# DeepNorm hybrid layer on one Trainium2 core: the first gate by seven half-size products inside the attention stage, the output gate's tiles in halves in the recurrence

## What is computed

```python
proj = x @ w_in
cq, ckv, kr, f_pre, q_pre, i_pre, g_pre, ga, gb = split(proj)      # ga, gb: 1024 columns each, g_pre: 512
a = attention(...)           # latent attention, softmax over earlier chunks (prompt) or a cache (sample)
o, S = hgrn2(...)            # gated linear recurrence over f, q, i
o = rms(o) * hg_norm * silu(g_pre)
merged = sigmoid(ga) * (a @ w_br_a) + sigmoid(gb) * (o @ w_br_b)
x = layernorm(ALPHA * x + merged @ w_out)
x = layernorm(ALPHA * x + mixture_of_experts(x) + sigmoid(x @ w_ple_gate) * (p @ w_ple))
```

## Time and profile before

| | us |
|---|---|
| median of 3 runs | 1517.29 (1516.72 to 1517.4) |
| profiled execution, device time | 1517.23 |
| its span, first to last instruction | 1515.5 |
| PE busy / DVE / ACT / POOL | 1273.6 / 453.6 / 287.0 / 62.8 |
| mean granted clock of TensorE | 0.918 |

### The profile page before, as it was taken

One profiled execution on the slowest core, in us unless ns is written; L12 is line 12 of the kernel. 1 busy time (PEld: TensorE's weight loads), 2 busy tenths in 40 slices (PEclk: granted clock), 3 DMA queues, 4 the chain that ended last, 5 costly groups with the idle time before them and its releaser, 6 DMA issues.

```text
span 1515.5 us, 21258 instructions
## 1 busy us (share of the span) xinstructions
PE 1273.6 (84%) x8912; PEld 738.4 (49%) x8913; DVE 453.6 (30%) x1109; ACT 287.0 (19%) x710; POOL 62.8 (4%) x102
## 2 busy tenths in 40 slices
PE   7999999999787767767799999999987876677664
PEld 4866897544332323322277679866442332333221
DVE  4552654532111101011166446445211111011003
ACT  3443422021001101001044434212111011000001
POOL 1300010000000000000040010000000000000000
PEclk9999999999899878788899999999998898778787
DMA  9503675999999999999972147679999999999994
GB/s 335 166 0 112 219 184 196 420 363 429 428 430 430 429 431 430 429 431 427 388 254 84 36 146 215 185 271 374 420 430 430 428 431 432 430 427 430 431 425 170
DMA packets 82643, 497.22 MB, mean 328 GB/s; under 512 B 7472, under 2 KB 13552, under 8 KB 51952
## 3 DMA queue, kind: packets, MB, share of 16 engines
q1 hardware_dynamic: 75392, 476.47, 76.7%
q0 software_dynamic: 7152, 19.32, 5.4%
HBM read 488.67 MB, written 2.89 MB: 324 GB/s over the span
## 4 chain that ended last, share of the span: by engine, by line
PE 57%; DMA 35%; DVE 3%; SPq 3%; issue 1%; ACT 1%; POOL 0%; DVEq 0%
PE bank L1105 55%; DMA ring<-in_w_e_up 7%; DMA ring<-in_w_e_down 5%; DMA ring<-in_w_e_gate 5%; DMA arena<-in_w_e_up 4%; DMA cst<-in_w_e_down 4%; DMA arena<-in_w_e_gate 4%; DMA cst<-in_w_e_gate 3%; DMA arena<-in_w_e_down 2%; SPq L924 2%; PE bank L1155 2%; DMA ring<-in_w_in 1%; SPq L985 0%; DVE arena L2304 0%; DVE arena L2144 0%
## 5 line engine op out<-in xcount | busy, mean ns | idle before, releaser
L1105 PE MATMUL bank<-arena 128*32 128x512 f32 (+11 forms) x2808 | 572.4, 540 | 169.6 <-DMA ring<-in_w_e_up 51.6
L1105 PE MATMUL bank<-ring,arena 128*32 128x512 f32 (+4 forms) x1360 | 422.2, 649 | 36.1 <-DMA arena<-in_w_e_gate 16.9
L1105 PEld LDWEIGHTS bank<-arena 128*32 128x32 f32 (+6 forms) x2808 | 210.5, 137 | 436.6 <-issue 422.9
L1105 PE MATMUL bank<-ring,xT 128*32 128x128 f32 (+5 forms) x1536 | 237.2, 363 | 1.3 <-ACT xT L1732 1.1
L1105 PEld LDWEIGHTS bank<-ring,xT 128*32 128x32 f32 (+1 forms) x1536 | 121.4, 137 | 100.6 <-issue 90.1
L1105 PEld LDWEIGHTS bank<-ring,arena 128*32 128x32 f32 (+1 forms) x1360 | 107.8, 130 | 123.1 <-issue 115.6
L1105 PE MATMUL bank<-xT,ring 128*128 128x144 f32 (+1 forms) x640 | 113.4, 335 | 0.0
L1105 PEld LDWEIGHTS bank<-xT,ring 128*128 128x128 f32 x640 | 95.1, 190 | 12.3
L1105 PE MATMUL bank<-arena,x_sb 128*128 128x128 f32 (+1 forms) x768 | 99.7, 282 | 1.4 <-DVE arena L2526 0.8
L1105 PEld LDWEIGHTS bank<-arena,x_sb 128*128 128x128 f32 (+1 forms) x768 | 90.5, 190 | 19.4 <-issue 12.7
L1105 PE MATMUL bank<-cst,arena 128*32 128x512 f32 x144 | 90.7, 789 | 0.0
(11 more groups left out here) (253 smaller groups left out, 1018.2 us busy)
## 6 DMA issues: line engine op xcount, KB each, us to landing
arena<-in_w_e_up SPq DMA_DIRECT2D x30, 2048.0 KB, 27.8
arena<-in_w_e_gate SPq DMA_DIRECT2D x28, 2048.0 KB, 27.1
ring<-in_w_e_gate SPq DMA_DIRECT2D x24, 2048.0 KB, 25.4
arena<-in_w_e_down SPq DMA_DIRECT2D x20, 2048.0 KB, 23.9
ring<-in_w_e_down SPq DMA_DIRECT2D x18, 2048.0 KB, 24.9
ring<-in_w_in SPq DMA_DIRECT2D x32, 1024.0 KB, 9.2
ring<-in_w_e_up SPq DMA_DIRECT2D x16, 2048.0 KB, 24.6
arena<-in_w_e_gate SPq DMA_DIRECT2D x16, 1024.0 KB, 14.4
```

The source lines that it names most:

```text
L1105: return pe.matmul(out, lhsT, rhs, start=first, stop=last, skip_group_check=True)
```

## The change

The first gate `ga` is made by the seven products too, in the attention stage: products 4 and 5 at the place of the output gate's first tile, 3 and 2 at that of the second, 7 and 1 behind the sample scores, 6 ahead of "lat". Their order is 4, 5, 3, 2, 7, 1, 6. POOL sums its weights by four accumulating DMAs behind the cache loads. Since its results need the room, the turned cache `cT` moves to the buffer of the forget gate and is loaded last, after the forget gate has been used. The output gate's tiles 0 and 1 go to four places of the recurrence's first tile, in halves of four matmuls (`HALF_AT` for first halves); its tile 2 stays. Product places of gb move up by one: each of the seven now has a place of its own. The ring's order of pieces changes: uq ahead of i, ga ahead of g.

```diff
-GATE_AT = {("ss",): [("ga", 0), ("ga", 1)], ("lat",): [("ga", 2)],
-           ("A", 0, 1): [("ga", 3)], ("A", 0, 3): [("ga", 4)], ("ks", 0): [("ga", 5)], ("o", 0): [("ga", 6)],
-           ("A", 1, 1): [("ga", 7)], ("A", 1, 3): seven_of("gb", 4), ("ks", 1): seven_of("gb", 5), ("o", 1): seven_of("gb", 3),
-           ("A", 2, 0): seven_of("gb", 2, 1), ("ks", 2): seven_of("gb", 7), ("o", 2): seven_of("gb", 6)}
+GATE_AT = {("at", 0): seven_of("ga", 4, 5), ("at", 1): seven_of("ga", 3, 2), ("ss",): seven_of("ga", 7, 1), ("lat",): seven_of("ga", 6),
+           ("A", 0, 3): [("g", 0)], ("o", 0): [("g", 1)],
+           ("A", 1, 1): seven_of("gb", 4), ("A", 1, 3): seven_of("gb", 5), ("ks", 1): seven_of("gb", 3), ("o", 1): seven_of("gb", 2),
+           ("A", 2, 0): seven_of("gb", 1), ("ks", 2): seven_of("gb", 7), ("o", 2): seven_of("gb", 6)}
+HALF_AT = {("A", 0, 1): 0, ("ks", 0): 1}
+SEVEN_ORDER = {"fq": SEVEN, "gb": SEVEN, "ga": (4, 5, 3, 2, 7, 1, 6)}
...
-    out += [(name, h) for name in ("cq", "kv", "f", "q", "i") for h in range(2)]
-    out += [("uq", 0), ("uq", 1), ("uk", 0), ("uv", 0)]
+    out += [(name, h) for name in ("cq", "kv", "f", "q") for h in range(2)]
+    out += [("uq", 0), ("uq", 1), ("i", 0), ("i", 1), ("uk", 0), ("uv", 0)]
+    out += [("ga", j, h) for j in range(2) for h in range(2)]
     out += [("g", 0), ("g", 1)]
-    out += [(name, j, h) for name in ("ga", "gb") for j in range(2) for h in range(2)]
+    out += [("gb", j, h) for j in range(2) for h in range(2)]
...
-    j += [("S", 1, n) for n in range(4)] + [("aT", 0), ("g", 0)] + [("PT", 1, kt, h) for kt in range(2) for h in range(2)]
-    j += [("ql",), ("aT", 1), ("i", 2), ("qlT",), ("g", 1)]
+    j += [("S", 1, n) for n in range(4)] + [("aT", 0)] + GATE_AT["at", 0] + [("PT", 1, kt, h) for kt in range(2) for h in range(2)]
+    j += [("ql",), ("aT", 1), ("i", 2), ("qlT",)] + GATE_AT["at", 1]
...
-        cT = carve(later_gates, 2, PAST)
-        wukT = carve(later_gates + 2 * PAST, HEADS, 2, 128)
+        cT = carve(H + 6144, 2, PAST)
+        wukT = carve(later_gates + T * FEATURES // 2, HEADS, 2, 128)
...
-                pool.dma_start(cT[:, :, :], cache_turned[layer]).then_inc(cache_in, 16)
...
+                pool.wait_ge(lf_out, 2 * (layer + 1))
+                pool.dma_start(cT[:, :, :], cache_turned[layer]).then_inc(cache_in, 16)
...
+                ns, w = quarters("ga")
+                pool.wait_ge(ring_full[SIGNAL_OF[ns[0, 1]]], 16 * FILLS[ns[0, 1]])
+                pool.dma_start(w[0, 1], from_input("ga", 1, 1), accum_op=ALU.add).then_inc(ga_sum[7], 16)
+                job_done(pool, (layer, "ga", 4, 1))
+                pool.dma_start(w[0, 0], from_input("ga", 0, 1), accum_op=ALU.add).then_inc(ga_sum[2], 16)
+                job_done(pool, (layer, "ga", 5, 1))
+                pool.wait_ge(ga_sum[2], 16 * (layer + 1))
+                pool.dma_start(w[1, 1], w[0, 0], accum_op=ALU.add).then_inc(ga_sum[1], 16)
+                job_done(pool, (layer, "ga", 3, 1))
+                pool.wait_ge(ga_sum[1], 16 * (layer + 1))
+                pool.dma_start(w[1, 0], w[1, 1], accum_op=ALU.add).then_inc(ga_sum[6], 16)
...
+                    if place in HALF_AT:
+                        project_half(layer, ("g",), HALF_AT[place], xT, [("g", 0), ("g", 1)], 0)
                     for name, *f in GATE_AT.get(place, []):
-                        if name == "gb" and len(f) == 2:
+                        if name == "g":
+                            project_half(layer, ("g",), f[0], xT, [("g", 0), ("g", 1)], 1)
+                        else:
                             seven((layer, name, *f), piece_number(layer, (name,) + SEVEN_WEIGHTS[f[0]]))
-                        else:
-                            by_features(layer, (name, f[0]), f[0] % 4, [(name, f[0] // 4, 0), (name, f[0] // 4, 1)], xT)
...
-                combined("g", (0,))
+                gates_at("at", 0)
...
-                combined("g", (1,))
+                gates_at("at", 1)
...
@@ ScalarE @@
-                        if name == "gb":
-                            if f[0] in (4, 5, 3):
-                                seven_copies(key, gb_copied)
-                            continue
-                        job_done(act, key)
-                        emptied(act.copy(dict(ga=gate_a, gb=gate_b)[name][f[0]], bank(key)[:, 0:T]), key)
+                        if name == "g":
+                            projected("g", hg, f[0], ACT.Copy)
+                        elif f[0] in (4, 5, 3):
+                            seven_copies((layer, name, *f), ga_copied if name == "ga" else gb_copied)
...
@@ VectorE @@
+                    if i == 1:
+                        gates_at("at", 0)
                     for kt in range(i + 1):
                         key = (layer, "PT", i, kt, 1)
                         job_done(dve, key)
                         emptied(dve.tensor_copy(probT[:, kt, 4:8, :], bank(key)[:, :].rearrange("p (h t) -> p h t", h=4)), key)
+                gates_at("at", 1)
...
+                gates_at("ss")
...
-                levels(0)
+                longer_sums(0, 0)
+                products(0, 0)
+                gates_at("lat")
+                levels(0, 1)
```

More of the change, by code:

```diff
@@ L709, in build @@
         hq_out = sem("hq_out")
+        ga_sum = {m: sem(f"ga_sum_{m}") for m in SUMS}
+        ga_copied = sem("ga_copied")
         gb_sum = {m: sem(f"gb_sum_{m}") for m in SUMS}
@@ L1045, in _, with quarters, from_input @@
                     pool.dma_start(kT[QK:QK + 2, h, :], masks[1]).then_inc(mask_in, 16)
+                pool.wait_ge(lf_out, 2 * (layer + 1))
+                pool.dma_start(cT[:, :, :], cache_turned[layer]).then_inc(cache_in, 16)
+                def quarters(name):
+                    ns = {(j, h): piece_number(layer, (name, j, h)) for j in range(2) for h in range(2)}
+                    return ns, {at: slot(n).rearrange("p (c n) -> p c n", c=4) for at, n in ns.items()}
+                def from_input(name, j, h):
+                    a = OFF[name][0] + 512 * j
+                    return w_in[layer].rearrange("(p c) n -> p c n", c=8)[:, 4 * h:4 * h + 4, a:a + 512]
+                ns, w = quarters("ga")
[9 more added lines that the diff above has]
+                pool.dma_start(w[1, 0], w[1, 1], accum_op=ALU.add).then_inc(ga_sum[6], 16)
                 job_done(pool, (layer, "ss", 2))
@@ L1050, in _ @@
                 pool.memset(att[:, :, :], 0.0).then_inc(zeroed, 1)
-                ns = {(j, h): piece_number(layer, ("gb", j, h)) for j in range(2) for h in range(2)}
-                w = {at: slot(n).rearrange("p (c n) -> p c n", c=4) for at, n in ns.items()}
-                def from_input(j, h):
-                    a = OFF["gb"][0] + 512 * j
-                    return w_in[layer].rearrange("(p c) n -> p c n", c=8)[:, 4 * h:4 * h + 4, a:a + 512]
+                ns, w = quarters("gb")
                 job_read(pool, (layer, "aTs"))
@@ L1181, in seven @@
                     pe.wait_ge(forms_out, layer + 1)
+                    if key[1] == "ga" and m in SUMS:
+                        pe.wait_ge(ga_sum[m], 16 * (layer + 1))
                     if key[1] == "gb" and m in SUMS:
@@ L1882, in _ @@
                 read_attended(0)
-                projected("g", hg, 0, ACT.Copy)
+                gates_at("at", 0)
                 read_probs(1)
@@ L1952, in gate_values @@
                     for k in pairs:
-                        if k < FEATURES // 2:
-                            for i in (2 * k, 2 * k + 1):
-                                job_read(act, (layer, "ga", i))
-                        else:
-                            job_read(act, (layer, "gb", 6 if k // 2 % 2 else 7, k % 2))
+                        name = "ga" if k < FEATURES // 2 else "gb"
+                        job_read(act, (layer, name, 6 if k // 2 % 2 else 1 if name == "ga" else 7, k % 2))
                         act.activation(gate_pair(k), gate_pair(k), ACT.Sigmoid).then_inc(early_gates, 1)
@@ L2209, in gather @@
                         dve.wait_ge(signal, copied(layer, m, p))
-                    job_read(dve, (layer, name, SEVEN[SEVEN.index(m) - 1], p))
+                    order = SEVEN_ORDER[name]
+                    job_read(dve, (layer, name, order[order.index(m) - 1], p))
                     for i, j, op in SEVEN_TO[m]:
@@ L2218, in gates_at @@
                     for name, *f in GATE_AT.get(place, []):
-                        if name == "gb" and f[0] != 4:
-                            gather((layer, name, *f), gb_copied)
+                        if name != "g" and f[0] != 4:
+                            gather((layer, name, *f), ga_copied if name == "ga" else gb_copied)
                 for t in range(3):
@@ L2402, in place_part, with levels @@
                         dve.sem_inc(att_out, 1)
-                def levels(t):
-                    for k in range(LEVELS[t]):
+                def levels(t, first=0):
+                    for k in range(first, LEVELS[t]):
```

21 lines of the change are left out of this document (13 added, 8 removed).

## The result

| | before | changed |
|---|---|---|
| median, 6 executions each | 1517.09 us (1516.37 to 1518.12) | 1507.06 us (1506.17 to 1507.89) |
| ratio | | 0.9932, 95% interval 0.9922 to 0.9942 |
| profiled execution, device time | 1517.23 | 1507.20 |
| span | 1515.5 | 1505.4 |

The change brings 10.0 us; 8.4 had been forecast (1508.8). In two later sessions the same kernel gave 1505.44 and 1508.01 us beside 1517.3 and 1517.8, gains of 11.9 and 9.8.

A forecast was written before the change was run, and what follows sets the result against it. Each layer was taken as a PE-bound part followed by a full expert-weight stream, with the change wholly in the first. Terms summed to -4.18 us a layer, -8.4 for two, so 1517.2 became 1508.8 us; range 1505.0 to 1513.0.

The forecast's parts named there:

- a microsecond behind 365 us is worth nothing: Expert stage: weights stream at full rate, so PE time saved there gains nothing; ahead of it, savings count one for one.
- attention, first and second place: Attention stage: two products, together 7.84 us, replace each output gate tile of 6.97 and 6.87 us; +0.87 and +0.97 us.
- wait for bank 0: Recurrence: PE's wait at the first level products for ACT to empty bank 0 goes; -0.25 us a layer.
- four half tiles: Recurrence: four output gate half tiles at 3.54 us replace four whole features, 14.16 for 15.67 us; -1.51 us a layer.
- wait before product 3: Recurrence: PE waits 1.14 us for DVE's gather of product 5, plus 0.16 restart; +1.30 us a layer, bounds 0 and 2.5.
- third tile's first place: Recurrence: product 1 alone at 3.92 us replaces products 2 and 1 with their 1.45 us wait, 9.54 us; -5.62 us a layer.
- Tile 0: Recurrence: slack of tile 0's attention weights before PE's outputs shrinks to 0.3 us; cost 0, up to 1 in the range.
- The sums: Attention stage: POOL's accumulating DMAs land in time, sum 2 with 5.7 us of slack before product 2; cost nothing.
- (1): Recurrence: DVE reaches the gather in time, no new wait; -5.5 us a layer, 1506.3 us, chance 0.17.
- (2): Recurrence: DVE becomes the bound and PE's shorter pieces turn into waits; -2.4 us a layer, 1512.4 us, chance 0.13.
- (3): Expert weights: their stream starts on something unmoved and absorbs the gain; 1515 to 1517 us, chance 0.07.
- (4): Attention stage: sum 2 is late and PE stands before product 2; at 22 us +2.8 a layer, 1522.8 us, chance 0.05.

The follow-up runs named there:

- e7: Changed kernel with the second branch's first feature made three times, +3.9 us of PE a layer just ahead of the expert weights; 1514.91 us, ratio 0.9984.
- e9: Kernel before with three branch features made from one of their four chunks each, 4.4 us of PE less a layer; 1508.52 us, ratio 0.9939.
- e10: Changed kernel with the second branch's first feature made twice, +1.96 us of PE a layer; 1510.99 us, ratio 0.9955.
- e8: Changed kernel with expert group 4's token gathering done twice, +6.4 us of PE a layer within the expert stream; 1508.46 us, ratio 0.994.
- e1_after: Changed kernel run again without any edit, as a yardstick; 1505.44 us, ratio 0.9922.
- e3: Changed kernel with all new places kept, but the first gate made by eight plain features without weight sums; 1517.07 us, ratio 0.9994.
- e6: Changed kernel without the first gate's four accumulating DMAs and PE's waits for them; 1505.56 us, ratio 0.9924.
- e2: Changed kernel with DVE's gather of second-gate product 5 moved ahead of tile 2's level 3, ACT's copies likewise earlier; 1503.26 us, ratio 0.9908.
- e4: Kernel before with first-gate feature 7 moved to "lat" and the second gate's product places moved up by one; 1515.44 us, ratio 0.9988.
- e11: Changed kernel run once more without any edit, on one chip with two other probes; 1508.01 us, ratio 0.9935.
- e5: Changed kernel with the accumulating DMA of the first gate's sum 2 issued twice, product 2 waiting for both; 1524.99 us, ratio 1.0053.

## Why the prediction was right

- **What bounds the kernel.** Confirmed by e7, e9 and e10, which moved the end by 9.5 for 7.8, 9.3 for 8.8 and 3.0 for 3.9 us of PE work in places with nothing of the gates. The sentence that a microsecond behind 365 us is worth nothing was only half right: in layer 0 of e8 the added work held nothing up, but the sentence left out PE's clock: the same block takes 7.11 or 8.80 us there, and the end moves with it. The waits on the chain are also not all "11 us and more": that of before has 11.32, 10.81 and 9.60 us one behind the other.
- **Terms of the sum, layer 0.** Measured as differences of starts on PE's timelines:

| term | forecast | measured |
|---|---|---|
| attention, first and second place | +0.87, +0.97 | +0.97, +0.97 |
| products 7 and 1, 6 | +0.02 | +0.12 |
| wait for bank 0 | -0.25 | -0.31 |
| four half tiles | -1.51 | -1.72 |
| first outputs | 0 | +0.10 |
| seventh place | +0.04 | +0.04 |
| wait before product 3 | +1.30 | +0.97 |
| third tile's first place | -5.62 | -5.61 |
| sum | -4.18 | -4.47 |

- Two terms were mis-sized by more than 0.1 us. The half tile is 3.49 us (13.95 for four), the value that half of the old tile had given; I had taken 3.54 between that and the output projection's. The wait was 0.93 instead of 1.14: DVE released the bank at G+18.0 as worked out (197.84 against G = 179.83, the start of the first outputs), but PE came at G+17.08 instead of 16.91, and the lost overlap was 0.07 instead of 0.16. Together they raise the gain by 0.54 us a layer. The first attention place, products 7, 1 and 6 and the first outputs take 0.1 us each of it back, and bank 0 gives 0.06. That leaves 4.47 a layer, 9.0 in all. The forecast's 8.4 against 10.0 is thus right in mechanism and a little small in size.
- **Layer 0 of this profile.** The terms add up to 4.47, yet the dense part is only 3.6 us shorter, because this execution took 0.85 us more from its first transpose to the first touched place (97.95 us against 97.10). The same kernel in e1_after took 97.19 there and is 4.4 shorter, so this is scatter ahead of the change.
- **Tile 0.** DVE's last copy of tile 0's weights ends at 179.72 and PE's outputs start at 179.83: of 0.3 us of slack 0.1 is left, and no wait, as had been taken. The outputs took 0.10 us more; e3 has this too, and its cause was not followed. **The sums.** Slack of sum 2 5.2 us against 5.7, cost nothing (e6). **The wait's place and cause.** As said; e2 took it away and got 2.2 us back.
- **What the forecast missed.** The gain of 9.8 to 11.9 in the medians is 1 to 3 us above these 9.0. The extra stands in the expert parts: their two stretches together are 1001.4 to 1002.0 us in the profiled executions of before, e3, e4 and e9, and 998.2 to 1000.4 in those of the changed kernel's kind (e8 apart). It isn't the earlier start, for e9 starts as early and has 1002.0. It is the clock of the two blocks told above. The forecast had taken this stage as the same in both kernels, which it is in bytes and work. Whether the change itself moves these blocks to the better is open. For it: the first block of layer 0 is slow in three of four profiles with eight gate features and in none of nine with seven products. Against it: one profile each, the last block of layer 1 is slow in the changed kernel's first profile too, and executions of one kernel scatter by 4 us (e11) to 5 us (e3, e7). The part of the gain beyond 9.0 us was not foreseen, and may be luck.
- **Rivals.** (1), no new wait, is what e2 built: its dense parts are 5.3 and 5.5 us shorter than before, close to the 5.5 worked out, and it ended at 1503.3, below the 1506.3, by its expert parts. The change itself has the wait, so this rival falls. (2), DVE as the bound: no, 0.1 us of slack held. (3), absorbed: no. (4), sum 2 late: did not occur, but its price was mis-sized. By my arithmetic an accumulate time of 20.8 us (9.15 and 11.67) would have left +1.6 us a layer against before; e5's dense parts show +4.7 and +6.1, and its median 7.4 in all against the 1517.6 beside it, because I had priced only the wait and not the lower clock behind it (2.9 and 2.5 us, and 1.7 more in layer 1).

## What to carry to other kernels

Find the point up to which PE paces the kernel and make the sum only ahead of it, piece by piece from start to start; here the terms added up to within 0.3 us a layer. Behind that point look at the blocks of PE work that stand between two waits for weights: their clock still moves the end, here by 1.3 to 2.2 us a block. When products move up by one place, follow each PSUM bank through the engine that empties it: here the wait did not vanish but went to another product, and moving one gather on DVE ahead of a level paid as much per layer as was waited. Price a wait on PE at its length plus what the following matmuls lose in clock; waits of 5.8 and 6.2 us cost another 2.9 and 2.5 here. Before a difference of 1 to 3 us in 1500 is given a cause, compare the pieces of several profiles.

## What the runs showed of the hardware

- After 5.78 us without work PE ran the next product in 7.00 us instead of 4.09, at a granted clock of 0.58; after 6.22 us in 6.58. After the waits of 0.93 us the product took 4.16 us, hardly more than 4.09, but once, in layer 1 of e5, 5.83 us at a clock of 0.70.
- In the expert stage the same block of 64 records took 7.11 us at a granted clock of 1.00, 8.80 at 0.81 and 9.55 at 0.74, and the last block of a layer 3.88 us at 1.00 or 5.50 at 0.69.
- The accumulate of 1 MB from HBM took 9.15 to 9.33 us where the DMA engines' share over its own time was 0.69 to 0.70 (112 to 115 GB/s), and 11.67 us where two other loads ran beside it (0.88, 211 GB/s). From slot to slot it took 7.52 us at a share of 0.69 and 8.92 at 0.87.
- Both gate forms cost what their columns say: two features at 288 columns 7.85 us, two products at 144 columns 7.84 to 7.94 us, and the products' weight loads fill the same time (PEld 7.94 us of 7.94) without a stall of PE.
